# A three-layer model on one core: the residual stream moves from feature order to token order

## The chip, the cores and the metric

The kernel runs on 1 core of a Trainium2 chip. The metric is the device time of one execution in microseconds (us). Lower is better. The core's engines are called PE (TensorE, matmuls; PEld is its weight loads), DVE (VectorE), ACT (ScalarE), POOL (GpSimd) and SP (the queue that issues most DMAs).

## The reference, cut to what matters

256 tokens of width 1024 pass two layers of one kind (`l` = 0, 1) and then one layer of another kind (the "second" part below), all in float32. Around the change the arithmetic of a layer is this:

```python
def rms_norm(x, g):
    y = x * lax.rsqrt(jnp.mean(x * x, axis=-1, keepdims=True) + EPS)
    return y * g

def hybrid_layer(x, mod, norm1, norm2, w_in, ..., w_out, w_ff1, w_ff2):
    shift1, scale1, gate1, shift2, scale2, gate2 = jnp.split(mod[:, None, :], 6, axis=-1)
    h = rms_norm(x, norm1) * (1.0 + scale1) + shift1
    proj = h @ w_in
    ...
    mix = jnp.concatenate([y_pool, y_nsa], axis=-1) @ w_out
    x = x + gate1 * mix
    h2 = rms_norm(x, norm2) * (1.0 + scale2) + shift2
    ff = jnp.square(jax.nn.relu(h2 @ w_ff1)) @ w_ff2
    return x + gate2 * ff
```

`mod` comes from a product of the condition vector with a weight of 1024 x 6144 per layer. The second part takes `x` into a state-space mixer, an attention and a gated output, adds `x` again under a layer norm, and ends with a feed-forward of the same size as the layers'.

## The kernel before

**Data.** Before the change `x` lies as `[128 features, 8 blocks kc, 256 tokens]`: a partition is a feature, so a gate, a shift or a gain is a per-partition scalar, and the sum of squares over features crosses partitions. Every matmul operand is split in two parts, `hi` (rounded to fp32r by ACT) and `lo` (the rest, subtracted by DVE), and a product is three matmuls, `hi*hi`, `hi*lo`, `lo*hi` (`mm3`, lines 422 to 424).

**Weights.** They arrive in panels of 1 MB through a ring of six slots (`load`, on SP). ACT makes the high part of a panel (`split_hi`, line 412), DVE the low part (`split_lo`, line 417), and PE uses it; `split_free` counts used panels and `used(k)` waits for one. 44 panels make a layer, counted 0 to 43: 8 and 9 are the half of `w_out` that takes the pooled features (`L_POOL`), 10 and 11 the half that takes the attention (`L_ATT`), 12 to 43 the feed-forward, in which an up panel and a down panel take turns.

**Order.** Each engine runs one instruction stream that is written out by hand in `pe_layer`, `act_layer` and `dve_layer`. What waits on an engine holds back all that stands behind it there. Between the stages DVE also reduces the condition's weight units (`mod(n)`, `dve_mod`, line 1145), two per turn, which a buffer pair takes from DMA; `dve_modc` then adds the bias and gives columns of `modc`.

**Two products of a layer have the weights stationary before the change.** `pe_out` (`w_out`) and `down` by way of `pe_panel_rows` (`w_ff2`) load 128 x 128 pieces of weights and stream 256 tokens. The second part's down projection already uses `pe_panel_tokens` (line 534): it loads 128 features of 128 tokens and streams 512 weight columns, and a panel is 8 `mm3` instead of 16.

**The norm.** There are four in the layers: `q` = 0 and 2 at the head of layers 0 and 1, `q` = 1 and 3 ahead of their feed-forwards. DVE adds the gated product to `x` block by block (lines 1371 and 1402), ACT squares (926), PE sums the squares with a matrix of ones (`pe_norm_sum`, 572), ACT makes the reciprocal root (920, 921), and then `dve_norm` and `act_norm` go over the eight blocks: DVE multiplies by gain and root (1173), ACT adds the shift and makes the high part (945), DVE the low part (1178). The first panel behind a norm takes the blocks as they come (`pe_head`, `pe_head_late`, and `up_head`, line 761).

**Where `x` is turned.** The input is turned to feature order by 16 transposes at the start. In the second part `x` is used as it is for the splits (1809, 1994) and for the `dt` product (1643), and it is turned back to token order for the layer norm (1743, copied by 1947).

Of the kernel before, what the change touches and what calls it, by code (L numbers as in the profile page):

```python
# [97 lines left out]
def build(nc, a, out, layers=DEPTH):  # L98
# [8 lines left out]
    with ctx:  # L107
# [5 lines left out]
        x = sb("x", [P, KC, T])  # L113
# [22 lines left out]
        rs = sb("rs", [P, T])  # L136
# [36 lines left out]
        x_turned = sem("x_turned")  # L173
# [3 lines left out]
        sq_added = sem("sq_added")  # L177
        ss_done = sem("ss_done")
        rs_done = sem("rs_done")
        t_done = sem("t_done")  # L180
# [62 lines left out]

        tbuf = area(KC * T, KC, T)
        y_at = at[0]
        ybuf = [area(2 * T, 2, T) for _ in range(3)]
# [49 lines left out]
        x_in = arena[:, q_at:q_at + TT * D].rearrange("p (t d) -> p t d", t=TT)  # L296
# [56 lines left out]
        def sp_layer(sp, l, ahead):  # L353
# [3 lines left out]
            def gate_mod(n):  # L357

                if n + 4 * (l > 0) < 12:
                    load_mod(sp, l, 8 + n + 4 * (l > 0))  # L360
# [25 lines left out]
            load_mod(sp, l, 20)  # L386
            load_mod(sp, l, 21)
# [15 lines left out]
            for u in (34, 35) if ahead else (22, 23):  # L403
                load_mod(sp, l, u)
# [143 lines left out]
        def pe_out(pe, m, k, steps=(0, 16)):  # L548
# [3 lines left out]
            att, c0 = divmod(k - L_POOL, 2)  # L552
            for i in range(*steps):
                c, kc = i // 4, i % 4
                n, s = 4 * c0 + c, kc * 512 + c * P
                last = mm3(bank[n // 2][:, (n % 2) * T:(n % 2 + 1) * T], wh[:, s:s + P], wl[:, s:s + P],
                           mix_hi[:, 4 * att + kc, :], mix_lo[:, 4 * att + kc, :],
                           att == 0 and kc == 0 and n % 2 == 0, att == 1 and kc == 3, skip=True)
# [5 lines left out]
        def pe_norm_sum(pe, q, kcs=range(KC), added=0):  # L564


            for kc in kcs:
                if added and kc == 0:
                    pe.wait_ge(sq_added, added)
                else:  # L570
                    pe.wait_ge(sq_done, KC * q + kc + 1)
                last = nc.tensor.matmul(bank[6][:, 0:T], ones, tbuf[:, kc, :], start=kc == 0, stop=kc == KC - 1)
            if kc == KC - 1:
                last.then_inc(ss_done, 1)

        def pe_layer(pe, l, ahead):
            m = 11 * l

            def arrive(kc):
                pe.wait_ge(act_ready, 16 * l + kc + 1)  # L580
# [132 lines left out]
            for g in range(4):  # L713
# [11 lines left out]
            pe_out(pe, m, L_POOL, (0, 4))  # L725
# [1720 lines left out]
```

## Time and profile before

| what | value |
|---|---|
| median of 3 executions | 1241.93 us (1240.52 to 1243.37) |
| span of the profiled execution, first to last instruction | 1239.2 us |
| mean clock granted to PE over the span | 0.982 of full speed |
| PE busy | 1169.2 us, 94% of the span |
| DVE busy | 912.1 us, 74% |
| ACT busy | 616.5 us, 50% |
| HBM read | 247.17 MB |

The profiled execution's time as the device measures it is not given apart; the median stands 2.7 us over its span. Busy times of PE count pipelined matmuls, so the duration of one matmul (283 ns for 256 columns) is more than the step from one start to the next. Where the text gives a cost of a PE instruction, it is that step.

### The profile page before, as it was taken

To read this page: it belongs to the slowest core of one execution; us is meant where nothing else is said; L and a number is where in the kernel's file an instruction comes from. 1 tells how busy PE (TensorE), PEld (TensorE's weight loads), DVE (VectorE), ACT (ScalarE), POOL (GpSimd) and SP (SyncE) were. 2 spreads that over 40 slices of the span, in tenths; PEclk is the share of its full clock that TensorE was granted. 3 is DMA by queue.
4 is the path that set the end of the run, shared out by engine and by line. 5 is a ranking of instruction groups with operands and counts; after the bars stand their busy time and mean duration, and the time that the engine had idled before them with its cause. 6 is when DMAs were issued, how large, how long until landed. Compare 5 with 4: busy or idle time off the path is not lost.

```text
span 1239.2 us, 19788 instructions
## 1 busy us (share of the span) xinstructions
PE 1169.2 (94%) x8054; PEld 1060.5 (86%) x8054; DVE 912.1 (74%) x1205; ACT 616.5 (50%) x814; POOL 58.5 (5%) x61
## 2 busy tenths in 40 slices
PE   3999999999999999999999998998989998999996
PEld 2878989999988888999999987887879997888885
DVE  6989798788778968756566479887984758656555
ACT  3663354434464435444444444568895733444441
POOL 1016000000001600000000000000000000000000
PEclk8999999999999999999999998999999999999999
DMA  9835568778765426555575533347854564555540
GB/s 382 365 142 208 201 229 300 270 273 294 263 218 204 170 69 241 179 184 191 175 265 196 175 132 103 118 164 245 263 200 137 186 225 167 170 182 191 191 148 34
DMA packets 44059, 249.35 MB, mean 201 GB/s; under 512 B 4352, under 2 KB 12672, under 8 KB 15952
## 3 DMA queue, kind: packets, MB, share of 16 engines
q1 hardware_dynamic: 43568, 246.19, 55.4%
q0 software_dynamic: 416, 2.11, 0.4%
q8 instruction: 54, 0.88, 0.3%
q14 instruction: 21, 0.17, 0.0%
HBM read 247.17 MB, written 1.11 MB: 200 GB/s over the span
## 4 chain that ended last, share of the span: by engine, by line
PE 78%; DVE 12%; ACT 5%; DMA 2%; issue 2%; SPq 0%; POOL 0%; DVEq 0%; ACTq 0%; POOLq 0%
PE bank L422 16%; PE bank L423 15%; PE bank L424 15%; PE bank L779 14%; PE bank L780 7%; PE bank L860 2%; DVE ring_w L417 2%; DMA raw<-in_panels 2%; DVE arena L2075 2%; PE bank L901 1%; ACT mixf L1894 1%; PE bank L761 1%; ACT mixf L1895 1%; PE bank L1681 1%; DMA arena<-in_modw 1%
## 5 line engine op out<-in xcount | busy, mean ns | idle before, releaser
L417 DVE TENSOR_TENSOR ring_w<-raw,w_hi 128x2048 fp32r<-128x2048 f32 x170 | 390.6, 2301 | 149.1 <-ACT w_hi L412 148.7
L412 ACT ACTIVATE w_hi<-raw 128x2048 fp32r<-128x2048 f32 x170 | 324.1, 1910 | 163.9 <-PE bank L424 152.7
L779 PE MATMUL bank<-act,w_hi 128*128 128x512 f32 x736 | 261.2, 397 | 0.2 <-DVE act L2212 0.2
L422 PE MATMUL bank<-act,w_hi 128*128 128x256 f32 x792 | 232.2, 293 | 7.3 <-DVE act L1178 2.7
L423 PE MATMUL bank<-act,w_hi 128*128 128x256 f32 x792 | 226.3, 286 | 0.0
L424 PE MATMUL bank<-act,ring_w 128*128 128x256 f32 x792 | 226.0, 285 | 0.0
L780 PE MATMUL bank<-act,ring_w 128*128 128x256 f32 x736 | 206.7, 281 | 0.0
L422 PEld LDWEIGHTS bank<-act,w_hi 128*128 128x128 f32 x792 | 154.3, 195 | 15.9 <-issue 13.3
L779 PEld LDWEIGHTS bank<-act,w_hi 128*128 128x128 f32 x736 | 138.6, 188 | 32.4 <-issue 0.5
L422 PE MATMUL bank<-ff_hi,w_hi 128*128 128x256 f32 (+1 forms) x560 | 157.7, 282 | 1.0 <-issue 1.0
L424 PE MATMUL bank<-ff_hi,ring_w 128*128 128x256 f32 (+1 forms) x560 | 158.2, 283 | 0.0
L423 PE MATMUL bank<-ff_lo,w_hi 128*128 128x256 f32 (+1 forms) x560 | 158.2, 282 | 0.0
L423 PEld LDWEIGHTS bank<-act,w_hi 128*128 128x128 f32 x792 | 154.3, 195 | 0.1
L424 PEld LDWEIGHTS bank<-act,ring_w 128*128 128x128 f32 x792 | 154.1, 195 | 0.0
L780 PEld LDWEIGHTS bank<-act,ring_w 128*128 128x128 f32 x736 | 139.5, 189 | 0.5
L1105 ACT ACTIVATE arena<-bank 128x256 f32<-128x256 f32 x96 | 36.8, 385 | 154.5 <-PE bank L780 150.8
L1145 DVE CUSTOM_DVE_ANT_0 arena<-arena,crow 128x1024 f32<-128x1024 f32 x88 | 106.0, 1243 | 10.2 <-DMA arena<-in_modw 9.9
L422 PEld LDWEIGHTS bank<-ff_hi,w_hi 128*128 128x128 f32 x560 | 106.5, 190 | 2.5 <-issue 1.1
L424 PEld LDWEIGHTS bank<-ff_hi,ring_w 128*128 128x128 f32 x560 | 106.6, 190 | 0.0
L423 PEld LDWEIGHTS bank<-ff_lo,w_hi 128*128 128x128 f32 x560 | 106.6, 190 | 0.0
L1437 DVE TENSOR_TENSOR arena<-bank,arena 128x256 f32<-128x256 f32 x96 | 39.8, 421 | 65.1 <-ACT arena L1105 65.1
L422 PE MATMUL bank<-mix_hi,w_hi 128*128 128x256 f32 x192 | 55.4, 289 | 0.0
(339 smaller groups left out, 1836.0 us busy)
## 6 DMA issues: line engine op xcount, KB each, us to landing
raw<-in_panels SPq DMA_DIRECT2D x170, 1024.0 KB, 4.8
arena<-in_modw SPq DMA_DIRECT2D x44, 1024.0 KB, 6.8
mixf<-dscr SPq DMA_DIRECT2D x8, 512.0 KB, 4.9
arena<-dscr SPq DMA_DIRECT2D x8, 512.0 KB, 5.3
mixf<-in_modw SPq DMA_DIRECT2D x2, 1024.0 KB, 15.6
act_flat<-in_modw SPq DMA_DIRECT2D x2, 1024.0 KB, 19.6
mixf<-dscr SPq DMA_DIRECT2D x8, 256.0 KB, 6.0
arena<-dscr SPq DMA_DIRECT2D x8, 256.0 KB, 6.6
```

Of the source, the lines that this page charges most:

```text
L412: nc.scalar.activation(w_hi[slot(k)][:, :], w_raw(m, k), ACT.Copy).then_inc(hi_done, 1)
L417: nc.vector.tensor_tensor(w_lo(m, k), w_raw(m, k), w_hi[slot(k)][:, :].bitcast(F32), ALU.subtract).then_inc(lo_done, 1)
L422: nc.tensor.matmul(o, wh, xh, start=start, stop=False, skip_group_check=skip)
L423: nc.tensor.matmul(o, wh, xl, start=False, stop=False, skip_group_check=skip)
L424: return nc.tensor.matmul(o, wl, xh, start=False, stop=stop, skip_group_check=skip)
L779: nc.tensor.matmul(bank[4 + c][:, :], wh[:, s:s + P], act2[:, kc, :, :], start=kc == 0, stop=False)
L780: last = nc.tensor.matmul(bank[4 + c][:, 0:T], wl[:, s:s + P], act_hi[:, kc, :], start=False, stop=kc == KC - 1)
L860: mm = lambda o, w, x, first=False, last=False: nc.tensor.matmul(o, w, x, start=first, stop=last, skip_group_check=True)
L1105: nc.scalar.activation(fr[par][:, c * T:(c + 1) * T], up_bank(at, c, final)[:, T:2 * T], ACT.Copy).then_inc(ff_cross, 1)
L1145: last = nc.vector.tensor_tensor_reduce(o, o, crow[:, :], 1.0, 0.0, ALU.mult, ALU.add, sums[:, col + b:col + b + 1])
L1437: nc.vector.tensor_tensor(fr[par][:, c * T:(c + 1) * T], up_bank(at, c, final)[:, 0:T], fr[par][:, c * T:(c + 1) * T], ALU.add).then_inc(f ...
L2075: ins = nc.vector.scalar_tensor_tensor(xb[:, b, :], src, w, xb[:, b, :], ALU.mult, ALU.add)
```

## The change

`x` is kept as `[128 tokens, 2 token blocks, 1024 features]`, a quarter being one token block and 512 features. In detail:

- `pe_out` and `down` of both layers load activations and stream 512 columns of weights. Their results come out in token order, quarter by quarter, in banks 0 to 3.
- The gate is now a value per column. PE turns the gate's columns of `modc` into rows in a bank (`pe_gate_row`, four transposes for a half), ACT copies them (`act_gate_row`), and DVE's update is a multiply and an add on a quarter (`dve_update`).
- ACT sums the squares by the accumulator of its Square (`act_stats`) and makes the root with small instructions; DVE scales the quarter (`dve_scaled`); PE turns it to feature order (`pe_features`); gain, shift, high part and low part follow, shared between ACT and DVE.
- The second part turns `x` for its splits, no longer turns it back, and makes its `dt` product with `mm3` on split operands.
- In layer 1 the units 20 and 21 of the condition's weights are loaded and reduced ahead of the feed-forward, two more turns of `mod` there and none at its end. The late gate columns are made before the feed-forward's last two steps. `split_lo(m + 11, 2)` and, ahead of `q` = 1 and 3, `split_lo(m, 13)` change their place.

```diff
-        def pe_out(pe, m, k, steps=(0, 16)):
+        def pe_out(pe, l, m, k, steps=(0, 8)):
...
+                tt, kc = i // 4, i % 4
+                if att:
+                    pe.wait_ge(mix_los, 4 * l + kc + 1)
+                ts, s = slice(tt * P, (tt + 1) * P), slice(512 * kc, 512 * (kc + 1))
+                last = mm3(bank[2 * tt + h][:, :], mix_hi[:, 4 * att + kc, ts], mix_lo[:, 4 * att + kc, ts], wh[:, s], wl[:, s],
+                           att == 0 and kc == 0, att == 1 and kc == 3, skip=True)
...
+        def pe_features(pe, src, arrived, base):
+            for n, (tt, _) in enumerate(quarters):
+                pe.wait_ge(arrived, base + n + 1)
+                for i in (0, 2, 1, 3):
+                    kc = 4 * (n % 2) + i
+                    last = nc.tensor.transpose(feature(kc)[:, tt * P:(tt + 1) * P], src[:, tt, kc * P:(kc + 1) * P], ident)
...
+        def pe_gate_row(pe, l, late, h, o):
+            pe.wait_ge(modc_ready, 4 * l + (4 if late else 2))
+            for c in range(4):
+                col = (40 if late else 16) + 4 * h + c
+                last = nc.tensor.transpose(o[:, c * P:(c + 1) * P], modc[:, col:col + 1].to_broadcast([P, P]), ident)
...
+            pe_gate_row(pe, l, False, 0, bank[7])
             pe_pv(pe, l, 4)
...
+            pe_out(pe, l, m, L_ATT, (0, 4)).then_inc(out_rows, 1)
+            pe_out(pe, l, m, L_ATT + 1, (0, 4)).then_inc(out_rows, 1)
+            pe_used(pe, pe_out(pe, l, m, L_ATT, (4, 8)))
+            pe_used(pe, pe_out(pe, l, m, L_ATT + 1, (4, 8)))
+            pe_features(pe, xn, y_ready, 8 * l + 4)
...
+        def act_stats(act, q, n):
...
+            nc.scalar.activation(xn[:, tt, cols], x[:, tt, cols], ACT.Square, accum_out=sq_sum[:, n:n + 1]).then_inc(sq_done, 1)
...
+            if n % 2 == 0:
+                nc.scalar.activation(sq_half[:, tt:tt + 1], sq_sum[:, n:n + 1], ACT.Identity, bias=cst[:, C_EPS:C_EPS + 1], scale=1.0 / D)
+            else:
+                nc.scalar.activation(sq_log[:, tt:tt + 1], sq_sum[:, n:n + 1], ACT.Ln, bias=sq_half[:, tt:tt + 1], scale=1.0 / D).then_inc(sq_done, 1)
+                act.wait_ge(sq_done, 8 * q + 4 * tt + 4)
+                nc.scalar.activation(rs[:, tt:tt + 1], sq_log[:, tt:tt + 1], ACT.Exp, scale=-0.5).then_inc(rs_done, 1)
...
@@ in act_norm
+            for pair in range(4):
+                kc = 2 * pair + 1
+                act.wait_ge(xt_full, 4 * q + feature_bank(kc) + 1)
...
+                nc.scalar.activation(hb[kc % 6], feature(kc), ACT.Identity, bias=modc[:, shift + kc:shift + kc + 1],
+                                     scale=gcol[:, g0 + kc:g0 + kc + 1]).then_inc(h_done, 1)
+                act.wait_ge(t_done, 4 * q + pair + 1)
+                nc.scalar.activation(act_hi[:, kc - 1, :], hb[(kc - 1) % 6], ACT.Copy).then_inc(act_his, 1)
+                act.wait_ge(h_done, 4 * q + pair + 1)
+                nc.scalar.activation(act_hi[:, kc, :], hb[kc % 6], ACT.Copy).then_inc(act_his, 1)
...
+            for n in range(3):
+                act_stats(act, 2 * l + 1, n)
             split_hi(act, m, 14)
+            act_stats(act, 2 * l + 1, 3)
...
+        def dve_update(dve, l, late, n):
...
+            nc.vector.tensor_tensor(xn[:, tt, cols], bank[n][:, :], grow[:, cols], ALU.mult).then_inc(upd_done, 1)
+            dve.wait_ge(upd_done, 8 * l + 4 * late + n + 1)
+            nc.vector.tensor_tensor(x[:, tt, cols], x[:, tt, cols], xn[:, tt, cols], ALU.add).then_inc(x_ready, 1)
+        def dve_scaled(dve, q, tt):
+            dve.wait_ge(rs_done, 2 * q + tt + 1)
+            for h in range(2):
...
+                nc.vector.tensor_scalar(xn[:, tt, cols], x[:, tt, cols], rs[:, tt:tt + 1], None, ALU.mult).then_inc(y_ready, 1)
...
@@ in dve_norm, scaled(kc): gain and shift of a block, from a bank
+            scaled(0)
+            for kc in range(KC):
+                if kc % 2 == 0 and kc < 6:
+                    scaled(kc + 2)
+                dve.wait_ge(act_his, 8 * q + kc + 1)
+                nc.vector.tensor_tensor(act_lo[:, kc, :], hb[kc % 6], act_hi[:, kc, :].bitcast(F32), ALU.subtract).then_inc(act_ready, 1)
...
+            split_lo(dve, m, 12)
+            update(0)
+            mod(10)
+            update(1)
+            mod(11)
+            dve_modc(dve, modc_ready, 4 * l + 3, 24, lc[:, LC_BM + 8:LC_BM + 24], MOD_PANELS * l + (22 if l else 20))
...
+            update(2)
+            dve_scaled(dve, 2 * l + 1, 0)
+            update(3)
+            dve_scaled(dve, 2 * l + 1, 1)
             dve_norm(dve, 2 * l + 1, KC, 24)
+            split_lo(dve, m, 13)
             split_lo(dve, m, 14)
...
+                split_lo(dve, m + 11, 2)
+            for n in range(4):
...
+                dve_update(dve, l, 1, n)
+                if ahead and n >= 2:
+                    dve_scaled(dve, 2 * l + 2, n - 2)
...
-                last = nc.tensor.matmul(bank[6][0:64, 0:T], lc2[:, L2_WDT + 64 * kc:L2_WDT + 64 * kc + 64], x[:, kc, :],
-                                        start=kc == 0, stop=kc == KC - 1)
+                last = mm3(bank[6][0:64, 0:T], ff_hi[:, 1, c], ff_lo[:, 1, c], act_hi[:, kc, :], act_lo[:, kc, :], kc == 0, kc == KC - 1)
...
-                                last = nc.tensor.transpose(bank[2 * tt + h][:, c * P:(c + 1) * P], x[:, 4 * h + c, tt * P:(tt + 1) * P], ident)
-                            last.then_inc(xk_turned, 1)
```

## Rows read from the trace of the kernel before

**Rows 1.** The page: busy by engine; one costly group (count, busy, mean ns).
```profile
PE 1169.2 (94%) x8054; PEld 1060.5 (86%) x8054; DVE 912.1 (74%) x1205; ACT 616.5 (50%) x814; POOL 58.5 (5%) x61
...
L412 ACT ACTIVATE w_hi<-raw 128x2048 fp32r<-128x2048 f32 x170 | 324.1, 1910 | 163.9 <-PE bank L424 152.7
```
**Rows 2.** The page: shares of the chain of work that ended last.
```profile
PE 78%; DVE 12%; ACT 5%; DMA 2%; issue 2%; SPq 0%; POOL 0%; DVEq 0%; ACTq 0%; POOLq 0%
```
**Rows 3.** Windows of one down panel: layer 0, then second part (busy by engine, clock).
```profile
244.68:250.42 5.74, 5.74 (x50) 5.74 (x49) 4.44 (x5) 2.71 (x3) 0.00 (x0) 1.00 0.55 186
1107.21:1112.68 5.47, 5.47 (x27) 4.51 (x25) 4.01 (x4) 2.71 (x3) 0.00 (x0) 1.00 0.58 193
```
**Rows 4.** Timeline of PE, second part: start, length, instruction, count.
```profile
716.25 3.67 PE L1643 MATMUL bank<-x,arena 128*64 128x256 f32 x16
...
954.27 1.91 PE L1743 MATMUL bank<-cst,x 128*128 128x128 f32 x16
955.93 0.36 PE L422 MATMUL bank<-act,w_hi 128*128 128x256 f32 x1
```
**Rows 5.** Timeline of DVE and PE at the start of layer 0.
```profile
39.33 2.28 DVE L417 TENSOR_TENSOR ring_w<-raw,w_hi 128x2048 fp32r<-128x2048 f32 x1
...
41.76 0.35 PE L422 MATMUL bank<-act,w_hi 128*128 128x256 f32 x1 [1.25 <-DVE ring_w L417]
```
**Rows 6.** Windows at the head panels of q = 1 and 3 (busy, clock).
```profile
165.00:168.30 3.30, 3.30 (x12) 2.82 (x11) 3.30 (x9) 2.17 (x5) 0.00 (x0) 0.50 0.41 174
480.30:482.00 1.70, 1.67 (x9) 1.39 (x10) 1.70 (x5) 1.02 (x2) 0.00 (x0) 1.00 1.00 421
```
**Rows 7.** Timeline of DVE and PE around q = 1, in layer 0.
```profile
153.13 1.23 DVE L1145 CUSTOM_DVE_ANT_0 arena<-arena,crow 128x1024 f32<-128x1024 f32 x1 [0.59 <-DMA arena<-in_modw]
...
162.05 0.88 DVE L1173 SCALAR_TENSOR_TENSOR arena<-x,gcol,rs 128x256 f32<-128x256 f32 x2
...
157.12 3.73 PE L572 MATMUL bank<-arena,cst 128*128 128x256 f32 x16
163.74 0.47 PE L761 MATMUL bank<-act,w_hi 128*128 128x512 f32 x1 [2.89 <-DVE act L1178]
...
170.97 0.39 PE L779 MATMUL bank<-act,w_hi 128*128 128x512 f32 x1
```
**Rows 8.** Timelines: single costs on DVE and ACT, of shapes near the new ones.
```profile
1225.30 0.69 DVE L2235 SCALAR_TENSOR_TENSOR arena<-arena,bank 128x512 f32<-128x512 f32 x1 [3.86 <-PE bank L424]
1226.03 0.69 DVE L2237 BATCH_NORM_STATS2 ln_st<-arena 128x6 f32<-128x512 f32 x1
...
724.89 0.62 DVE L2055 TENSOR_SCALAR arena<-arena,small 128x768 f32<-128x768 f32 x1
...
663.69 2.77 DVE L1994 TENSOR_TENSOR act<-x,act 128x256 fp32r<-128x256 f32 x8
...
158.39 1.59 ACT L926 ACTIVATE arena<-x 128x256 f32<-128x256 f32 x4 [3.59 <-DVE x L1371]
...
724.47 0.18 ACT L1828 ACTIVATION_READ_ACCUMULATOR arena<-arena,small 128x1 f32 x1
```
**Rows 9.** Timeline of DVE and PE around q = 2, at the head of layer 1.
```profile
340.92 2.29 DVE L417 TENSOR_TENSOR ring_w<-raw,w_hi 128x2048 fp32r<-128x2048 f32 x1
...
352.73 0.55 PE L422 MATMUL bank<-act,w_hi 128*128 128x256 f32 x1 [2.69 <-DVE act L1178]
...
360.02 0.28 PE L422 MATMUL bank<-act,w_hi 128*128 128x256 f32 x1
```
**Rows 10.** Timeline of PE at q = 3 and at the start of the second part.
```profile
475.25 2.32 PE L572 MATMUL bank<-arena,cst 128*128 128x256 f32 x10
480.33 0.47 PE L761 MATMUL bank<-act,w_hi 128*128 128x512 f32 x1 [2.75 <-DVE act L1178]
...
486.48 0.39 PE L779 MATMUL bank<-act,w_hi 128*128 128x512 f32 x1
...
664.25 0.36 PE L422 MATMUL bank<-act,w_hi 128*128 128x256 f32 x1 [1.39 <-DVE act L1994]
```

More of the change, by code:

```diff
@@ L402, in sp_layer @@
             e = m + FF_STEPS // 2 - 1
[L403 removed]
+            for u in (34, 35) if ahead else ():
                 load_mod(sp, l, u)
@@ L562, in pe_used @@
             last.then_inc(split_free, 1)
[L564 to L574, printed above, removed]
+        def pe_features(pe, src, arrived, base):
[4 more added lines that the diff above has]
+                    last = nc.tensor.transpose(feature(kc)[:, tt * P:(tt + 1) * P], src[:, tt, kc * P:(kc + 1) * P], ident)
+                    if tt and i >= 2:
+                        last.then_inc(xt_full, 1)
+        def pe_gate_row(pe, l, late, h, o):
[3 more added lines that the diff above has]
+                last = nc.tensor.transpose(o[:, c * P:(c + 1) * P], modc[:, col:col + 1].to_broadcast([P, P]), ident)
+            last.then_inc(grow_mm, 1)
         def pe_layer(pe, l, ahead):
@@ L809, in pe_ff @@
             e = m + FF_STEPS // 2 - 1
+            if not second:
+                for h in range(2):
+                    pe_gate_row(pe, l, True, h, bank[6 + h])
             up(e, k0 + 1, j0 + FF_STEPS - 1, 1)
@@ L1114, in step, with rows, ff_schedule @@
                     split_hi(act, mm, s[1])
-            ff_schedule(act, m, k0, j0, step, final)
+            def rows():
+                for h in range(2):
+                    act_gate_row(act, l, True, h, bank[6 + h])
+            ff_schedule(act, m, k0, j0, step, final, between=None if final else rows)
         def up_bank(at, c, final):
             return bank[c if not final and isinstance(at, int) and at == 0 else 4 + c]
-        def ff_schedule(eng, m, k0, j0, step, final):
+        def ff_schedule(eng, m, k0, j0, step, final, before=None, between=None):
             step(m, j0, k0, 0, None, (k0 + 3, k0 + 4), 0)
@@ L1417, in mod @@
                 if mods and not inside and at < 2:
-                    turn = 0
+                    turn = 0 if mods == "ahead" else 1
                 elif mods == "ahead":
                     turn = at if inside else 7
-                elif mods == "tail" and not inside:
-                    turn = 1
                 else:
@@ L1942, in act_second @@
                     nc.scalar.activation(rs2, rs2, ACT.Exp, scale=-0.5).then_inc(y_rs, 1)
-                if i == 6:
-                    for n in range(4):
-                        act.wait_ge(xk_turned, n + 1)
-                        nc.scalar.activation(xtok[:, n // 2, 512 * (n % 2):512 * (n % 2 + 1)], bank[n][:, :], ACT.Copy).then_inc(xk_taken, 1)
                 if i in (6, 7):
@@ L2308, in _ @@
                     last.then_inc(c_turned, 1)
[L2309 to L2315 removed]
             pe.wait_ge(cact_ready, 2)
+            pe_features(pe, xn, y_ready, 0)
             for l in range(layers):
```

296 lines of the change are left out of this document (134 added, 162 removed).

## The prediction, made before the changed kernel was run

> **What bounds the kernel.** I read the page first: PE is busy 94% of the span, and the chain that ended last lies on PE for 78% of it and on DVE for 12% [rows 1, 2]. So two things count: the step of PE's matmuls in the long stretches, and the handovers between stages, where the chain leaves PE for DVE and ACT. The change touches both. For the first I took windows of one down panel in either form [rows 3] and PE's timeline for single operations [rows 4]. For the second I read the timelines of DVE, ACT and PE at the start and at the norms [rows 5, 7, 9, 10], the granted clock there [rows 6], and durations of similar shapes [rows 8]. In the fast stretches the clock is 1.00, which is the 2.4 GHz level; 0.50 is the 1.2 GHz level.
>
> **Products with activations stationary.** A down panel in today's form is 48 matmuls of 256 columns and takes 5.74 us; the same panel in the new form, as the second part runs it, is 24 of 512 columns and takes 5.47 [rows 3]. That is 0.27 us a panel. A layer has 16 down panels and 4 panels of `w_out`. I count 14 down panels in layer 0 (the last two lie in the norm's sum below) and 16 in layer 1: 30 x 0.27 = -8.1 us. The eight panels of `w_out` are 8 x 0.27 = 2.2 us, but those of layer 0 end ahead of a norm that does not wait for them (below), and those of the pooled half are used up by gate rows.
>
> By the Trainium skill, page "TensorE: Matmul & The Clock Gate", section "Back-to-back issue gap", an isolated matmul steps by its columns at 2.4 GHz and 2.5 ns, which would make both forms of a panel equal within 0.1 us, and the sum would be 6 us higher (a rival below). The trace differs: the windows show 119.6 ns a step for 256 columns and 227.9 for 512, and the smaller one pays more over its streaming time.
>
> **Gate rows.** Transposes step by 1.66/16 = 0.104 us (16 of them between two starts) [rows 4]. Each layer gets 16. The first four come where PE waits for DVE anyhow. The next four cost 0.4 us and the pooled half's two panels give 0.5: nothing. The late eight stand between two panels in a stretch where PE never waits: 2 x 0.83 = +1.7 us. DVE's gate columns for them come a whole panel earlier, so no wait is added.
>
> **The start, q = 0.** PE's second panel waits for `split_lo` that DVE starts at 39.33 [rows 5]. Ahead of it DVE did 16 instructions for the norm at 0.4 us (two took 0.88) [rows 7]; it will do 12, eight of them plain subtractions at 2.77/8 = 0.35 [rows 8], and statistics, scaling and transposes lie under the condition's DMAs. ACT gets 12 instead of 8 at 0.4 us [rows 8], and then bounds: I get the last low part 1.5 us earlier, so -1.5. If ACT's extra four are wholly exposed it is 0; a gain over 1.7 is excluded, since the first panel's own matmuls end then.
>
> **Costs of the new norm chain** [rows 8]. Update of a quarter: multiply and wait 0.73, add 0.61, together 1.34 us. Statistics behind a second quarter: Square of 512 columns 0.62, accumulator read 0.18, Ln and Exp like it 0.2 each: 1.2. Scaling: a 768-column tensor-scalar takes 0.62, so a 512-column one about 0.4, two 0.8. Then transposes 0.5, one block from the bank (0.4), two high parts (0.8), one low part (0.35) before PE may start. From the last update's end that is about 4.2 us; ACT and DVE then give all blocks in 12 x 0.4 = 5 us. Nothing in the trace is Square with a second output; I take its bound below as 0.62 and above as the 0.8 with the read, which differ by 0.2 a norm.
>
> By the Trainium skill, "VectorE: DVE Perf Modes", section "Why PSUM operands drop a tier", float32 tensor-scalar goes at double rate only between SBUF tensors. The trace agrees: 768 columns took 0.62, less than 512 took in an instruction with two tensors (0.69). By that rule the scaling is cheap where it stands; scaling at single rate would add 0.4 us a norm.
>
> **The clock behind a pause.** At q = 1 the head panel ran 3.3 us at 0.50 soon after PE had paused 3 us; at q = 3 the clock stayed 1.00 behind a like pause [rows 6]. In the slow case a head panel takes 7.2 us from its first matmul (163.74 to 170.97; at q = 2, 352.73 to 360.1, much the same), against 6.2 at q = 3 where the blocks set the pace [rows 7, 9, 10]. The new pauses are 6 to 11 us with a few transposes in them, so I take 7.2 for q = 1 and 2. Faster blocks would give 5.7 at a full clock.
>
> **q = 1.** DVE is late here, not PE: the tenth mod turn starts at 153.13, when its DMA lands, while `w_out` runs until 157.12 [rows 7]. From there: turn 2.3, update 1.34, turn 2.3, columns 0.4, update 1.34 (160.8), scaling 0.8, update 1.34. ACT does the third quarter's statistics (to 161.9), then `split_hi` 14 as it is ordered, 1.9 us [rows 1] (to 163.8), then the last statistics (165.0). Scaling to 165.8; PE starts at 167.9 and ends the head at 175.1, against 170.97: +4.1 us. `split_lo` 13, now behind the norm, ends about 174.0 and is hidden by 1 us; at a full clock it is what PE waits for, and the cost is +2.7.
>
> **q = 2.** DVE ends its last feed-forward split at 343.2 [rows 9]; columns 0.3, the moved `split_lo` 2.2 (345.7), updates to 349.7, scaling 350.5, last update 351.9, statistics 353.1, scaling 353.9, transposes and features to a first matmul at 356.1 against 352.73. With 7.2 us the head ends at 363.3, against 360.1: +3.2 us, at a full clock +1.7. Today the updates come first and the split hides in the norm; moved ahead, it is exposed, which is most of this.
>
> **q = 3.** PE ends `w_out` about 474.7. The two moved mod turns fill a pause in which DVE waited for PE. The third update starts when the third half-panel step is done (472.1), the last at 474.9; 4.2 us behind its end (476.3), first matmul at 480.4 against 480.33, head end 486.1 or, at the slow clock, 487.6, against 486.48 [rows 10]: -0.4 or +1.1. I take +0.4.
>
> **The second part.** Its first matmul came 1.5 us behind the last down panel [rows 10]. Now an update (1.34), transposes and a bank's split stand there, and the blocks come in fits: +0.7 us. The `dt` product was 3.6 us and becomes 24 matmuls at 0.12: -0.7. Its operands are split early. The 16 transposes of `x` back go: -1.7 [rows 4].
>
> **Sum.** -8.1 + 1.7 - 1.5 + 4.1 + 3.2 + 0.4 + 0.7 - 0.7 - 1.7 = -1.9 us. The changed kernel's span would be 1239.2 - 1.9 = 1237.3; the median stands 2.7 over the span, so 1240.0 us.
>
> **Rivals and chances.** What a measurement of this kernel tells from no change is about 0.2%, 2.5 us: faster is under 1239.4, slower over 1244.4.
> - The forecast, 45%, own range 1238 to 1243: a third of it under 1239.4.
> - The norms cost less: the clock stays at 1.00 at q = 1 to 3, as it did at q = 3. Each slow head saved is 1.4 to 1.5 us: 1240.0 - 1.4 - 1.5 - 0.8 = 1236.3. For it speaks q = 3, against it the longer pauses. 20%.
> - The start and the norm chains turn out much shorter than my sums because ACT and DVE overlap better, and the norms lose nothing: 1232 to 1235. 12%.
> - Slower: the norm chain hands over between DVE, ACT and PE some six times, and each handover costs more than the 0.03 to 0.1 us I gave it. At 0.3 us more, four norms and the second part add 5 x 6 x 0.3 = 9 us less what the slow clock hides, about 6: 1246. It decides from 0.2 us a handover. The rows of chained pairs speak against it. 18%.
> - The step of 512 columns in the layers, where DVE and ACT work more beside PE than in the second part, falls back to twice that of 256 less a quarter of today's difference: 2 us saved in place of 8.1, so 1246. The windows of the second part speak against it. This is near what the Trainium skill's page "TensorE: Matmul & The Clock Gate", section "Back-to-back issue gap", would give. 5%.
>
> Chances: faster 0.45, same 0.33, slower 0.22. The range runs from 1233.5 to 1247, which leaves out the ends of the last three.
>
> **What would show it.** Right: down panels of 5.47 us in the layers; `split_lo` for the second panel at about 37.8; head panels ending 4, 3 and 0.5 us later against the panels before them; the two rows of the transposes back gone. Wrong: a first FF matmul at q = 1 before 166 or behind 170; idle time of PE inside the feed-forward behind a late `split_lo` 13 or 14, since DVE leaves the norm 4.7 us later than today and PE only 4; a clock of 1.00 in the heads.

## The result, and the profile after

| | before | after |
|---|---|---|
| median (17 runs each) | 1242.33 us (1239.57 to 1248.25) | 1244.54 us (1242.66 to 1247.19) |
| span of the profiled execution | 1239.2 us | 1242.1 us |

The ratio after to before is 1.0022, 95% interval 1.0012 to 1.0031: the change costs 2.7 us, 1.5 to 3.9 by the interval. The forecast was 1240.0, a gain of 1.9 us. A second set of the changed kernel (11 runs, the last experiment) gave 1.0029 (1.0016 to 1.0042).

I set the two traces side by side at places that both have, and noted how far the changed kernel is behind at each. The last column adds the prediction's terms up to that place (for q = 2: 2.6 - 3.8 + 0.8 + 3.2).

| place on PE | before | after | behind | forecast |
|---|---|---|---|---|
| second panel of layer 0 | 41.76 | 40.88 | -0.9 | -1.5 |
| head panel of q = 1 ends | 170.97 | 176.87 | +5.9 | +2.6 |
| head panel of q = 2 ends | 360.02 | 368.28 | +8.3 | +2.8 |
| head panel of q = 3 ends | 486.48 | 495.81 | +9.3 | +3.2 |
| second part's first matmul | 664.25 | 671.53 | +7.3 | +0.4 |
| end of the span | 1239.2 | 1242.1 | +2.9 | -1.9 |

So the loss is made at q = 1 and q = 2; the rest of the program gives back more than forecast. The changed kernel's page answers to [rows 1, 2]: PE is busy 10 us less, and the end is later all the same.

```profile
PE 1158.9 (93%) x7130; PEld 1012.3 (81%) x7130; DVE 916.0 (74%) x1192; ACT 622.1 (50%) x851; POOL 58.5 (5%) x61
...
PE 77%; DVE 11%; ACT 5%; DMA 3%; issue 2%; SPq 0%; POOL 0%; DVEq 0%; ACTq 0%; POOLq 0%
```

The products came as forecast. Windows of the changed kernel over three down panels in layer 0 (columns as in [rows 3]) show 5.47 us each at a clock of 1.00, where [rows 3] had 5.74.

```profile
182.52:187.99 5.47, 5.47 (x26) 4.51 (x25) 5.44 (x8) 2.19 (x2) 0.00 (x0) 1.00 0.58 192
193.66:199.13 5.47, 5.47 (x27) 4.51 (x25) 5.44 (x6) 2.83 (x3) 0.00 (x0) 1.00 0.98 373
326.94:332.41 5.47, 5.47 (x27) 4.46 (x25) 4.16 (x5) 2.71 (x3) 0.00 (x0) 1.00 1.01 428
```

The norms did not. The timeline of PE in the changed kernel at q = 1, then at q = 2, answers to [rows 7, 9]. The bracket gives the idle time ahead of an instruction and what ended it. L585 are the transposes, in two groups of eight with a pause ahead of each; L785 and L435 are the first matmuls of the heads.

```profile
161.72 1.97 PE L585 MATMUL bank<-cst,arena 128*128 128x128 f32 x8 [5.94 <-DVE arena L1224]
165.89 1.97 PE L585 MATMUL bank<-cst,arena 128*128 128x128 f32 x8 [2.21 <-DVE arena L1224]
168.58 0.76 PE L785 MATMUL bank<-act,w_hi 128*128 128x512 f32 x1 [0.72 <-DVE act L1242]
...
353.52 1.09 PE L585 MATMUL bank<-cst,arena 128*128 128x128 f32 x8 [3.62 <-DVE arena L1224]
357.08 1.97 PE L585 MATMUL bank<-cst,arena 128*128 128x128 f32 x8 [2.47 <-DVE arena L1224]
360.10 0.55 PE L435 MATMUL bank<-act,w_hi 128*128 128x256 f32 x1 [1.05 <-DVE act L1242]
```

At q = 1 the form before had 6.6 us from the end of `w_out` (157.12) to the head's first matmul, 3.7 of them filled with norm sums [rows 7]. Now it is 13.0 us (from 155.6). The transposes take 1.97 us for eight where the clock is down and 1.09 where it is not. Windows of the changed kernel over the first part of each head (q = 1; q = 2 from the transposes on; q = 3) answer to [rows 6]:

```profile
168.60:174.30 5.70, 5.70 (x18) 4.83 (x19) 5.51 (x11) 2.88 (x9) 0.00 (x0) 0.50 0.00 0
357.08:364.90 7.82, 6.76 (x30) 6.39 (x31) 5.25 (x14) 6.43 (x14) 0.00 (x0) 0.50 0.40 163
488.72:492.10 3.38, 3.38 (x11) 2.94 (x12) 3.19 (x10) 2.89 (x9) 0.00 (x0) 0.55 1.01 416
```

The clock is 0.50 for 5.7 us and for 7.8 us, where [rows 6] had it for 3.3, and q = 3 is slow, which was fast before. The heads take 8.3, 8.2 and 7.1 us; before they took 7.2, 7.3 and 6.2.

DVE and ACT at q = 1, changed kernel. L1196 is a turn of `mod`, L1215 and L1217 are the multiply and the add of an update, L1224 is the scaling, L425 is ACT's `split_hi` and L946 the Square of the statistics:

```profile
153.53 1.23 DVE L1196 CUSTOM_DVE_ANT_0 arena<-arena,crow 128x1024 f32<-128x1024 f32 x1 [2.41 <-DMA arena<-in_modw]
...
161.97 0.68 DVE L1215 TENSOR_TENSOR arena<-bank,arena 128x512 f32<-128x512 f32 x1
162.69 0.69 DVE L1217 TENSOR_TENSOR x<-x,arena 128x512 f32<-128x512 f32 x1
165.35 0.88 DVE L1224 TENSOR_SCALAR arena<-x,rs 128x512 f32<-128x512 f32 x2 [1.97 <-ACT rs L954]
...
162.25 1.89 ACT L425 ACTIVATE w_hi<-raw 128x2048 fp32r<-128x2048 f32 x1
164.05 0.61 ACT L946 ACTIVATE arena<-x 128x512 f32<-128x512 f32 x1
```

DVE stands 2.41 us for a modulation unit. The last update ends at 163.3, but ACT is splitting panel 14 until 164.1, so the last statistics start 0.7 us late, and DVE's scaling stands 1.97 us in all. Three candidates follow: what stands in DVE's and ACT's order, the landing, and the clock.

### The profile page after: what moved, and what is told of

It is laid out like the page before. It is cut to its first block, busy times and chain, and to the rows that moved or that the text cites. A ratio compares the mean times of both kernels' runs of the same rounds, so it can differ in the third digit from the quotient of the medians.

```text
span 1242.1 us, 18002 instructions
## 1 busy us (share of the span) xinstructions
PE 1158.9 (93%) x7130; PEld 1012.3 (81%) x7130; DVE 916.0 (74%) x1192; ACT 622.1 (50%) x851; POOL 58.5 (5%) x61
## 4 chain that ended last, share of the span: by engine, by line
PE 77%; DVE 11%; ACT 5%; DMA 3%; issue 2%; SPq 0%; POOL 0%; DVEq 0%; ACTq 0%; POOLq 0%
PE bank L435 15%; PE bank L436 15%; PE bank L437 15%; PE bank L803 14%; PE bank L804 7%; PE bank L882 2%; DMA raw<-in_panels 2%; DVE ring_w L430 2%; DVE arena L2126 2%; PE bank L923 1%; ACT mixf L1947 1%; PE bank L785 1%; ACT mixf L1948 1%; PE bank L1739 1%; DMA arena<-in_modw 1%
## 5 line engine op out<-in xcount | busy, mean ns | idle before, releaser
L425 ACT ACTIVATE w_hi<-raw 128x2048 fp32r<-128x2048 f32 x170 | 324.3, 1911 | 159.3 <-PE bank L437 144.6
L435 PE MATMUL bank<-act,w_hi 128*128 128x256 f32 x792 | 231.9, 293 | 3.6 <-ACT arena L1980 2.0
L435 PEld LDWEIGHTS bank<-act,w_hi 128*128 128x128 f32 x792 | 153.9, 194 | 12.2 <-issue 9.5
L435 PE MATMUL bank<-w_hi,ff_hi 128*128 128x512 f32 x384 | 149.9, 390 | 0.0
L436 PE MATMUL bank<-ring_w,ff_hi 128*128 128x512 f32 x384 | 149.9, 390 | 0.0
L437 PE MATMUL bank<-w_hi,ff_lo 128*128 128x512 f32 x384 | 149.4, 389 | 0.0
L1196 DVE CUSTOM_DVE_ANT_0 arena<-arena,crow 128x1024 f32<-128x1024 f32 x88 | 105.9, 1243 | 12.3 <-DMA arena<-in_modw 11.9
L435 PEld LDWEIGHTS bank<-w_hi,ff_hi 128*128 128x128 f32 x384 | 72.1, 188 | 15.9
L437 PEld LDWEIGHTS bank<-w_hi,ff_lo 128*128 128x128 f32 x384 | 72.1, 188 | 15.4
L436 PEld LDWEIGHTS bank<-ring_w,ff_hi 128*128 128x128 f32 x384 | 72.1, 188 | 13.3
L2126 DVE SCALAR_TENSOR_TENSOR arena<-arena 128x256 f32<-128x256 f32 x96 | 39.1, 479 | 9.7 <-ACT arena L1897 9.7
```

The source lines that it names most:

```text
L425: nc.scalar.activation(w_hi[slot(k)][:, :], w_raw(m, k), ACT.Copy).then_inc(hi_done, 1)
L435: nc.tensor.matmul(o, wh, xh, start=start, stop=False, skip_group_check=skip)
L436: nc.tensor.matmul(o, wh, xl, start=False, stop=False, skip_group_check=skip)
L437: return nc.tensor.matmul(o, wl, xh, start=False, stop=stop, skip_group_check=skip)
L1196: last = nc.vector.tensor_tensor_reduce(o, o, crow[:, :], 1.0, 0.0, ALU.mult, ALU.add, sums[:, col + b:col + b + 1])
L2126: ins = nc.vector.scalar_tensor_tensor(xb[:, b, :], src, w, xb[:, b, :], ALU.mult, ALU.add)
```

## The experiments

All are edits of the changed kernel unless the heading says otherwise. Each was timed beside the kernel before on the same chip; the ratio is to that kernel, so 1.0022 is "no better than the change". That kernel's own median moved between the sets (1242.33, then 1241.16, 1241.23 and 1240.95 us), so what an edit gained is read from the difference of two ratios, 0.001 being 1.24 us, and not from two medians. Each ratio has an interval of 0.001 to 0.002 to either side, so a gain of under 2 us is seen in the traces and not in the times alone.

### 1. The moved split, back behind the norm

```diff
-                split_lo(dve, m + 11, 2)      # ahead of the late updates
...
-            if l == 0:
-                split_lo(dve, m, 2)
+            split_lo(dve, m, 2)               # behind dve_norm, in both layers
```

> The changed kernel, but the low part of layer 1's third panel stands behind the second norm again (q = 2) and no longer ahead of the late updates. Theory (the moved instruction is serial in front of the norm): updates, statistics, transposes and PE's head all come 2.2 us earlier at q = 2; the head's first matmul 10.4 us behind the end of the last feed-forward panel today becomes 8.2, so the median falls by 2.2 us, from 1244.5 to 1242.3. Rival (the late updates wait for PE's last down panel, so the split is hidden): less than 0.7 us. Rival (the norm's loss is in the handovers and the clock, whatever stands ahead): no change in PE's pauses of 3.6 and 2.5 us, they only start elsewhere.

Measured: 1242.28 us, ratio 1.0010 (1.000 to 1.002). PE's timeline of this kernel at q = 2, from the last down panel's last matmul:

```profile
348.98 0.39 PE L437 MATMUL bank<-w_hi,ff_lo 128*128 128x512 f32 x1
350.78 1.09 PE L585 MATMUL bank<-cst,arena 128*128 128x128 f32 x8 [1.42 <-DVE arena L1224]
354.34 1.97 PE L585 MATMUL bank<-cst,arena 128*128 128x128 f32 x8 [2.47 <-DVE arena L1224]
357.36 0.55 PE L435 MATMUL bank<-act,w_hi 128*128 128x256 f32 x1 [1.05 <-DVE act L1242]
```

The first pause is 1.42 us and not 3.62, and the head starts 8.4 us behind that matmul and not 10.6: -2.2, as the theory had it. The pauses behind it are unchanged to 0.01 us. The split was serial. The ratios differ by 1.5 us, and their intervals overlap: the time agrees with 2.2 us but does not show it by itself.

### 2. The modulation units ahead of panel 15

```diff
-            load(sp, m, 15)
             gate_mod(10)
             gate_mod(11)
+            load(sp, m, 15)
```

> The changed kernel, but panel 15 of each layer is fetched behind the two last modulation units, not ahead of them. Theory (at q = 1 the chain is pinned by the landing of unit 18, which shares the DMA queue with panel 15): the eleventh mod turn starts at about 151.1 us and not at 153.5, when DVE is through with what stands ahead of it, and all behind it up to the head panel comes 2.4 us earlier; the median falls by 2.4 us to 1242.1. Rival (the landing was not what bound, or the freed time goes into PE's pause ahead of the norm and the next unit lands late instead): under 0.5 us. At q = 3 nothing changes in either case, since DVE is not late there.

Measured: 1241.89 us, ratio 1.0003 (0.9994 to 1.0013), 2.4 us better than the change. DVE's timeline of this kernel at the unit's turn:

```profile
150.90 1.22 DVE L1196 CUSTOM_DVE_ANT_0 arena<-arena,crow 128x1024 f32<-128x1024 f32 x1
```

The turn starts at 150.90 without a wait, and the head's first matmul at 165.95, 10.5 us behind the end of `w_out` (155.5) and not 13.0: -2.5. The head at q = 3 was slow for longer in this profile, 8.5 us against 7.1, which is why the span (1239.9) shows less than q = 1 gained.

### 3. Statistics ahead of ACT's split, both scalings behind the last update

```diff
-            for n in range(3):
+            for n in range(4):
                 act_stats(act, 2 * l + 1, n)
-            split_hi(act, m, 14)
-            act_stats(act, 2 * l + 1, 3)
             act_norm(act, l, 2 * l + 1, 24, KC)
+            split_hi(act, m, 14)
...
             update(2)
-            dve_scaled(dve, 2 * l + 1, 0)
             update(3)
+            dve_scaled(dve, 2 * l + 1, 0)
             dve_scaled(dve, 2 * l + 1, 1)
...
-                if ahead and n >= 2:
-                    dve_scaled(dve, 2 * l + 2, n - 2)
+            if ahead:
+                dve_scaled(dve, 2 * l + 2, 0)
+                dve_scaled(dve, 2 * l + 2, 1)
```

> The changed kernel, but in both norms inside a layer ACT does the last statistics ahead of the split of panel 14, and at q = 1 to 3 DVE scales the first half of the tokens behind the last update, not ahead of it. Theory (each instruction between the last update and the transposes is on the path, handovers are cheap): at q = 1 -1.5 us (last update 0.8 earlier, and ACT 0.7 earlier than the split let it), at q = 2 -0.8, at q = 3 nothing, since the last update waits for PE there: together -2.3 us, median 1242.2. Rival (the slow clock sets the head's end, not the first matmul): first matmuls earlier by the same, but the heads longer by as much, median within 0.5 of 1244.5.

Measured: 1239.40 us, ratio 0.9984 (0.9975 to 0.9993), about twice the gain of the theory. The chain gave what was expected (first matmul -1.2 us at q = 1, -0.65 at q = 2). The rest goes with the clock, and not with the rival's sign: the heads at q = 2 and 3 are short. In all 12 executions the mean clock over the span is 0.983 to 0.987, where the changed kernel had 0.977 to 0.981 in all of its 28, so this is not the chance of one profile. Timeline of PE and two windows of this kernel at q = 2, the 16 transposes and the head:

```profile
352.88 3.44 PE L585 MATMUL bank<-cst,arena 128*128 128x128 f32 x16 [4.83 <-DVE arena L1223]
357.61 0.35 PE L435 MATMUL bank<-act,w_hi 128*128 128x256 f32 x1 [1.28 <-DVE act L1241]
```

```profile
352.88:356.30 3.42, 3.42 (x16) 3.21 (x16) 2.13 (x5) 1.30 (x6) 0.47 (x1) 0.55 1.02 429
357.61:363.43 5.82, 5.82 (x48) 5.82 (x49) 4.02 (x9) 4.63 (x10) 0.00 (x0) 1.00 0.12 48
```

At q = 2, with one pause in place of two, the slow stretch falls on the transposes, and the whole head runs at 1.00: 5.8 us, not 8.2. At q = 1 it does not come out so: behind one pause of 7.24 us the 16 transposes take 3.67 us, and the head, at a mean clock of 0.74, still takes 7.4 us.

### 4. PE kept busy in the pauses

```diff
+        def warm(n, o):
+            for _ in range(n):
+                nc.tensor.matmul(o[:, :], mix_hi[:, 2, 0:P], mix_hi[:, 0:2, :], start=True, stop=True)
...
             for n, (tt, _) in enumerate(quarters):
+                if n == 0:
+                    warm(pads[0], bank[4])
+                if n == 2:
+                    warm(pads[1], bank[0])
                 pe.wait_ge(arrived, base + n + 1)
...
+            warm(pads[2], bank[2])
```

> The changed kernel with matmuls added whose result nobody uses, in PE's pauses at q = 1, 2 and 3 (24, 15 and 0 ahead of the first transposes, 9 between the two groups of transposes, 3 behind them; 0.23 us each). The output is unchanged. Theory (the slow clock behind the longer pauses is a third of what the change lost): heads and transposes run at 1.00; eight transposes take 1.0 us and not 2.0, the head at q = 1 takes 5.8 us and not 8.3, at q = 2 5.8 and not 8.2, at q = 3 5.8 and not 7.1: about -6 us in all less what the blocks' pace gives back (1 us a norm), median 1240 to 1241. Rival (the blocks that DVE and ACT hand over set the head's pace, the clock is hidden by it): under 1 us in all. Rival (the added matmuls delay the transposes): slower by up to 2 us.

Measured: 1239.80 us, ratio 0.9990 (0.998 to 1.000). Windows of this kernel over the three whole heads, and over a stretch of layer 1:

```profile
168.31:173.96 5.65, 5.65 (x33) 4.85 (x33) 5.45 (x11) 3.02 (x10) 0.00 (x0) 1.00 0.00 0
357.58:363.41 5.83, 5.83 (x48) 5.83 (x49) 4.04 (x9) 4.62 (x10) 0.00 (x0) 1.00 0.09 38
485.06:490.79 5.73, 5.73 (x33) 4.95 (x33) 5.53 (x11) 3.00 (x10) 0.00 (x0) 1.00 0.77 323
400.04:415.35 15.31, 14.81 (x99) 12.55 (x99) 12.71 (x25) 9.16 (x13) 1.47 (x2) 0.89 0.00 0
```

The heads are 2.6, 2.4 and 1.4 us shorter: 6.3 us is what the slow clock took from them in the changed kernel's profile. The time fell by less, 4.0 us by the ratios. Two things are seen: behind the heads of q = 1 and 3 the next up panel takes 6.3 to 6.4 us in place of 5.65, since PE now waits for DVE's splits, and in this execution the clock fell behind another pause, at 400 (0.89 in the last row), which cost 1.35 us (the same stretch takes 13.96 us in the changed kernel). In all 12 executions the mean clock over the span is 0.988 to 0.991. The clock is a price of its own, and the blocks' pace does not hide it.

### 5. The same padding in the kernel before

The `warm` of run 4, with 11 matmuls behind `pe_norm_sum` at q = 1 and 3 and 18 at q = 2, in the kernel before.

> The kernel before, with matmuls added whose result nobody uses, behind its norm sums at q = 1 and 3 (11) and at q = 2 (18); the output is unchanged. It prices the slow clock in the form before. Its heads at q = 1 and 2 took 7.2 and 7.3 us and at q = 3 6.15; the changed kernel with the like padding had 5.65, 5.83 and 5.73. Theory (both forms pay the slow clock, the changed one 6.3 us and the one before 3.3 us): heads of 5.7 to 6.2 us here, -1.2, -1.3 and -0.2, less 0.5 given back behind each of the first and third, where PE waits for the first down panel: -1.5 to -2.5 us, median 1239 where the kernel before has 1241.2. Rival (the blocks' pace sets the head in the form before, as its steps of 0.7 us a block at q = 3 suggest): within 1 us of the kernel before. Slower would say that the padding delays the blocks.

Measured: 1240.37 us, ratio 1.0001 (0.998 to 1.002). Its windows over the three heads:

```profile
165.18:171.33 6.15, 6.15 (x32) 1.00 0.44 187
354.47:360.22 5.75, 5.75 (x49) 1.00 0.62 257
480.54:486.70 6.16, 6.16 (x33) 1.00 0.83 350
```

At a clock of 1.00 the heads at q = 1 and 3 take 6.15 us, so the blocks set their pace, and the slow clock cost the form before 1.1 us at q = 1, at most 1.5 at q = 2 and nothing at q = 3: 2.6 us. At q = 2 the padding was too long and put the head's start 1.2 us later, which ate most of its gain and may have let more blocks be ready: in the profile of run 9, the same form without padding, that head ran at 1.00 by itself and took 6.2 us (353.12 to 359.31), so the slow clock's price there may be 1.1 and the sum 2.2. The time is of little help here, as its interval of 2.5 us to either side holds the theory and the rival; by the heads the rival is near the truth: the form before had little to win. Over the whole span the two forms' clocks differ less than over the three heads: the median of the mean clocks is 0.981 before and 0.980 after, since each has slow stretches elsewhere too.

### 6. Runs 1 to 3 together

> The changed kernel with the edits of the first three runs together: the low part of layer 1's third panel behind the norm, the two modulation units ahead of panel 15, statistics ahead of the split of panel 14 and both scalings behind the last update. Theory (these are serial pieces of one chain and add up): first matmuls earlier by 2.5 + 1.2 us at q = 1, by 2.2 + 0.65 at q = 2, nothing at q = 3; with heads as in the third run -1.6, -2.0 and -4.5 add to -8.1 less what PE then waits for behind the heads (0.7): 1244 - 7.4 = 1236.5 where the kernel before has 1241.2. Rival (the pieces hide one another, or the clock eats what the chain gives): 1239 to 1240, like the third alone.

Measured: 1234.67 us, ratio 0.9947 (0.9933 to 0.9960), 6.6 us under the kernel before. Timeline of PE at q = 1 in this kernel:

```profile
155.54 0.39 PE L437 MATMUL bank<-w_hi,mix_lo 128*128 128x512 f32 x1
160.71 3.48 PE L585 MATMUL bank<-cst,arena 128*128 128x128 f32 x16 [4.78 <-DVE arena L1223]
165.10 0.47 PE L785 MATMUL bank<-act,w_hi 128*128 128x512 f32 x1 [0.92 <-DVE act L1241]
```

From the end of that first matmul, 155.8, to the head it is 9.3 us in place of 13.0, and at q = 2 7.5 in place of 10.6. The pieces add up: they stood one behind another. At q = 2 the head stayed slow, though the two pauses ahead of it were shorter than in run 3:

```profile
347.24 1.12 PE L585 MATMUL bank<-cst,arena 128*128 128x128 f32 x8 [2.64 <-DVE arena L1223]
348.68 1.97 PE L585 MATMUL bank<-cst,arena 128*128 128x128 f32 x8 [0.32 <-DVE arena L1223]
```

```profile
351.70:358.99 7.29, 7.29 (x48) 7.29 (x49) 7.07 (x10) 4.74 (x10) 0.00 (x0) 0.77 0.44 183
```

### 7. Run 6 with the padding

Pads of (22, 0, 3), (11, 0, 4) and (8, 0, 4) at q = 1, 2, 3.

> The run above with matmuls added whose result nobody uses: 22 ahead of the transposes and 3 behind them at q = 1, 11 and 4 at q = 2, 8 and 4 at q = 3. The output is unchanged. Theory (clock and chain are separate prices): 16 transposes take 1.8 us and not 3.5, the heads 5.7; against the run above that is -1.7 -1.7 at q = 1, -1.7 at q = 2 and about -0.5 at q = 3, less 0.7 given back behind a head: 1232 to 1234. Rival (what PE then waits for is DVE's splits behind the norm): the same as without, 1236.

Measured: 1232.86 us, ratio 0.9934 (0.9920 to 0.9948). Every head runs at 1.00 (5.73, 5.82, 5.73 us). That lies in the theory's 1232 to 1234, but by luck: the gain over run 6 is 1.8 us and not some 5, and run 6 stood at 1234.67 and not at the 1236.5 it was reckoned from. Run 6 had only one slow head left (q = 2, 7.3 us) and slow transposes. The two runs' intervals overlap.

### 8. The scalings alone

The second hunk of run 3 without the first.

> The changed kernel with one edit alone: both scalings stand behind the last update at q = 1 to 3, so that PE gets all 16 transposes in one stretch; ACT's order is as in the changed kernel. It tells what of the third run's -4.5 us came from the clock. Theory (one pause in place of two, and the clock is slow for less of the head): the first matmul at q = 1 no earlier by more than 0.1 (ACT's split holds the statistics), at q = 2 0.65 earlier; the head at q = 2 5.8 us and not 8.2, at q = 3 5.7 and not 7.1, at q = 1 about 7.4: in all -3 to -4 us, median 1240 to 1241. Rival (that was chance in one profile and the chain alone counts): -0.8 us, median 1243.

Measured: 1240.79 us, ratio 0.9994 (0.998 to 1.0007), 3.5 us better than the change by the ratios (4.3 by the second set of the change). Windows of this kernel: transposes and head at q = 2, heads at q = 3 and q = 1:

```profile
355.30:358.74 3.44, 3.40 (x16) 2.68 (x16) 2.21 (x5) 1.59 (x7) 0.46 (x1) 0.57 1.00 424
359.75:365.58 5.83, 5.83 (x49) 5.83 (x49) 4.04 (x9) 4.62 (x10) 0.00 (x0) 1.00 0.17 67
486.03:491.68 5.65, 5.65 (x33) 4.85 (x33) 5.45 (x11) 3.02 (x10) 0.00 (x0) 1.00 0.80 331
169.10:177.43 8.33, 8.33 (x32) 7.14 (x33) 7.60 (x11) 2.98 (x10) 0.00 (x0) 0.65 0.00 0
```

At q = 2 and 3 this is the theory's pattern to 0.1 us. At q = 1 it is not: the head took 8.33 us and not 7.4, as slow as in the changed kernel, though there too both scalings stand behind the last update. Only 0.9 us of the gain is the chain at q = 2; most comes from where the slow clock falls. In all 11 executions the mean clock is 0.982 to 0.985, again above each of the changed kernel's 28, which rules out the rival's chance.

How long the head is slow does not follow from the number of pauses alone. The rows of runs 3, 6 and 8, one profile each:

| place | PE's pauses ahead of the transposes | clock over the transposes | head |
|---|---|---|---|
| q = 3, runs 3 and 8 | 1.91 and 0.35 to 0.37 us | 1.00 | 5.7 us at 1.00 |
| q = 2, run 6 | 2.64 and 0.32 us | falls between the two groups | 7.3 us at 0.77 |
| q = 1, run 6; q = 2, runs 3 and 8 | 4.78 to 4.84 us | 0.55 to 0.57 | 5.7 to 5.8 us at 1.00 |
| q = 1, runs 3 and 8 | 7.24 us (run 8: 0.89 more) | 0.50 | 7.4 and 8.3 us at 0.74 and 0.65 |

### 9. The modulation units first, in the kernel before

The edit of run 2 in the kernel before.

> The kernel before, with panel 15 fetched behind the last two modulation units: the second run's edit in the other form. It tells whether the landing that pinned q = 1 belongs to the change or to both forms. Theory (both are pinned by it, but the form before less, since its last four updates also wait for the output projection's end at 157.1): first matmul at q = 1 1 to 1.5 us earlier, median 1239.9 where the kernel before has 1241.2. Rival (the form before is bound by the projection alone there): within 0.3 us.

Measured: 1242.22 us, ratio 1.0005 (0.9991 to 1.0018), the rival's number. DVE at the unit's turn and PE at the head in this kernel:

```profile
153.12 1.21 DVE L1145 CUSTOM_DVE_ANT_0 arena<-arena,crow 128x1024 f32<-128x1024 f32 x1
164.17 0.72 PE L761 MATMUL bank<-act,w_hi 128*128 128x512 f32 x1 [2.76 <-DVE act L1178]
```

The turn starts where it did in [rows 7], now without the wait of 0.59 us. But in this profile PE and DVE were 0.67 us late well ahead of the edit's place (the first update at 149.35 and not 148.68; the clock was 0.50 and not 0.66 from 20 to 40 us), so the places are compared with the end of `w_out`: the head comes 6.4 us behind it (157.79 to 164.17) in place of 6.6. The landing cost the form before 0.2 us, and the changed one, whose DVE stood at the unit 2.41 us, 2.5. So nearly all of the landing is a price of the change.

### 10. Panel 14's low part later

```diff
             split_lo(dve, m, 13)
-            split_lo(dve, m, 14)
...
-                if s[0] is not None:
+                early = not final and isinstance(at, int) and at == 0
+                if early:
+                    split_lo(dve, mm, k0 + 2)
+                elif s[0] is not None:
                     split_lo(dve, mm, s[0])
                 dve.wait_ge(ff_his, jn + 1)
...
+                if early:
+                    split_lo(dve, mm, s[0])
```

> The seventh run's kernel (all edits and the padding), with the low part of panel 14 made inside the first feed-forward step, while DVE waits for ACT's high part, and that of panel 15 behind the step's own low part. Theory (with the heads at full clock, PE's wait of 0.7 us ahead of the first down panel at q = 1 and 3 is DVE's order behind the norm): the second up panel takes 5.65 us and not 6.3 at both places, -1.3 us, 1231.6 where the seventh run's kernel had 1232.9. Rival (ACT's split of panel 15 holds the high part anyway): -0.3 us or less.

Measured: 1232.73 us beside run 7's 1232.86; ratio 0.9925 (0.9903 to 0.9946), whose interval holds run 7's. The second up panel does take 5.6 us, but the first down panel is followed by a wait of the same 0.7 us: the next step's sum on DVE comes at 181.59, and the third up panel starts at 182.16:

```profile
181.59 0.75 DVE L1496 TENSOR_TENSOR arena<-bank,arena 128x256 f32<-128x256 f32 x2
182.16 0.47 PE L812 MATMUL bank<-act,w_hi 128*128 128x512 f32 x1 [0.59 <-DVE arena L1496]
```

From the head's end to that wait's end the two orders are equal to about 0.2 us (170.37 to 182.16, and 170.03 to 181.96 in run 7). DVE has no wait between 170.70 and 181.59 in this trace: its total there is what binds, so the rival's number holds, though not its reason.

### 11. The changed kernel once more

> The changed kernel once more, for a second profile: how long the clock is slow differs from one execution to the next. Theory (the first matmuls' places are fixed by the chain, the heads' lengths by where the slow clock falls): 12.8 to 13.1 us from the end of the output projection to the head at q = 1 and 10.5 to 10.6 at q = 2; heads between 7.0 and 8.5 us at q = 1 and 2, between 5.7 and 8.5 at q = 3; median 2 to 3.5 us over the kernel before.

Measured: 1244.75 us, ratio 1.0029 (1.0016 to 1.0042). From the end of `w_out` to the head 13.0 us, and 10.6 from the last down matmul at q = 2. The median is 3.8 us over the kernel before in this set, just outside the theory. Windows over its heads:

```profile
169.48:177.76 8.28, 8.28 (x32) 0.65 0.00 0
360.83:369.10 8.27, 8.27 (x49) 0.66 0.03 8
489.54:496.61 7.07, 7.07 (x32) 0.78 0.64 267
```

The same three lengths as in the first profile. But run 1, whose code at q = 1 is the same, had a head of 7.0 us there. By the Trainium skill, page "TensorE: Matmul & The Clock Gate", section "What's actually happening", the cold stretch varies from run to run for one kernel. The runs agree: 8.3, 8.3 and 7.0 us at q = 1, and at q = 3, where run 2's head starts as long behind `w_out` as the changed kernel's (5.98 and 5.99 us), 7.1, 7.1 and, in run 2, 8.5.

## Why the prediction was wrong

**The products, right.** From the end of a feed-forward's head to the end of its last down panel the changed kernel gains 3.2 us in layer 0 (176.1 to 172.9) and 3.4 in layer 1, the late gate rows included; 16 panels at 0.27 less 0.8 are 3.5. The rival that the 512-column step falls back in the layers is out: 5.47 us in each window. By the Trainium skill, page "TensorE: Matmul & The Clock Gate", section "Back-to-back issue gap", both forms of a panel would by my estimate from its formula take equal time within 0.1 us; the windows here show 5.74 and 5.47 us.

**The start, right on DVE, wrong on PE.** DVE's `split_lo` for the second panel starts at 37.81, 1.5 us earlier, as forecast. PE's second panel comes only 0.9 earlier, since its first panel started at 32.92 and not at 31.93 and now ends last.

**The step that failed: q = 1, with q = 2 behind it.** The sum gave the norm at q = 1 +4.1 us and a start's gain of 1.5 beside it; in the profile all up to there is +5.9. Of the 4.8 us between the forecast and the profile, q = 1 has 3.3, q = 2 has 2.2 and q = 3 has 0.6, and the rest of the program gave 1.3 back.
- 1.5 us is an error of the sum. I started the chain of q = 1 at 153.13, when a DMA lands, and got +4.1 against the kernel before at a fixed time. A time that a landing pins holds nothing of what was gained earlier, so the start's -1.5 must not be added to it; up to there the forecast is +4.1. Runs 2 and 9 showed the pin: 2.5 us in the changed kernel, 0.2 in the one before.
- 1.1 us is the head: 8.3 and not 7.2. I took the length from heads of the form before, where PE had run 16 norm sums ahead of its pause. Run 4 showed that the slow clock costs the three heads 6.3 us; run 5 showed at most 2.6 in the form before. I had noted the longer pauses and still kept the old number.
- 0.7 us is the chain. The unit landed at 153.53 and not 153.13, and the eight transposes behind the last scaling took 1.97 us at the low clock, where I gave 0.5; the rest was shorter than its terms.
- The sign I had set for this step, a first matmul before 166 or behind 170, did not show it: the matmul came at 168.58. What did show it are the heads' ends against the panels before them, forecast 4, 3 and 0.5 us later and found 6.8, 5.6 and 1.0.

At q = 2 the moved `split_lo` cost the forecast's 2.2 us (run 1). The head was 1.0 us over (8.2), the chain 0.8: the transposes again, and the head there waits for the low parts of two blocks, not one. At q = 3 the head was slow, the worse of the two cases I had written; +1.0 and not +0.4.

**The rest of the kernel, better than forecast.** The second part's first matmul lost 1.4 and not 0.7 us. `dt` gave 0.7. The transposes back gave 1.7, and before them another 1.5 us was won by chance of the clock: in the kernel before the panel behind a pause at 920 took 7.3 us, in the changed one 5.85. It is no gain of the change, since in run 9 and in run 5, which keep the form before, that panel took 5.86 us too. From the second part's first matmul to the end -4.4 us, forecast -2.4.

**The rivals.** None of them was it. The slower one had the right side (1246) by the wrong cause: from one engine to the next it is 0.04 us (the addition at q = 2 starts at 354.49 and takes 0.69, ACT's square starts at 355.22) to 0.1, and run 6 won 9 to 10 us against the change without removing a handover. "The clock stays at 1.00" went the other way: it was slow for longer, and at q = 3 too.

**What stays open.** Why one pause left the head slow at q = 1 (runs 3 and 8) and not at q = 2 isn't known; each row is one profile, and no run changed the length of a pause alone. Why the clock in run 4 fell behind a pause at 400 that left it alone in the changed kernel and in runs 1 to 3 isn't known either.

## What to carry to other kernels

Where a change makes PE pause, the pause can be paid twice, since the clock may be low behind it (here 6.3 us over three heads against 2.2 to 2.6 before). Try one pause in place of two, with PE's small work behind it in one piece and the large work last: it won 3.5 us here (run 8), at two norms of three, and did not help at the third. Look at the granted clock over the large work in each place, since neither the length nor the number of the pauses foretold it. And let nothing on DVE or ACT stand between the last update and the first use that can stand behind it (run 6: 0.9947 of the kernel before, where the change alone is 1.0022). In a forecast, mark each time that a DMA landing pins: a gain made ahead of it ends there.

## What was not expected of the hardware

- Nearly the same idle time can leave the clock slow for very different lengths. With 3.6 + 2.5 + 1.1 us of pauses (changed kernel, q = 2) PE ran at 0.50 for 7.8 us; with 4.8 + 1.3 us (run 3) it was slow for no more than 3.4 us, all of it on transposes. And with only 2.6 + 0.3 + 1.1 us (run 6) a head was slow.
- A unit of 1 MB whose DMA shared the queue with a panel issued ahead of it and a unit issued 2.3 us later took 8.2 us to land (issued 145.3, DVE ended its wait at 153.5); with the panel behind both units it was issued at 145.2 and DVE had it by 150.90, at most 5.7 us later (run 2).
